# Projections pa and pb of a hybrid trunk: from plain block products to seven products per column pair, in sequence with the gates

## The reference

```python
hn = rms_norm(h, norm_g[l])
z = jnp.einsum("btd,dn->btn", hn, w_in[l])
xa, sa, vb, gb, sb, ma, mb = jnp.split(z, SPLIT_IDX, axis=-1)
ya = rg_lru(causal_depthwise_conv(xa, ...), ...) * jax.nn.silu(sa)
pa = jnp.einsum("btc,cd->btd", ya, w_proj_a[l])
yb = causal_depthwise_conv(vb * jax.nn.sigmoid(gb), ...)
yb = jax.nn.silu(layer_norm(yb, ...)) * jax.nn.silu(sb)
pb = jnp.einsum("btc,cd->btd", yb, w_proj_b[l])
merged = jax.nn.sigmoid(ma) * pa + jax.nn.sigmoid(mb) * pb
h = h + jnp.einsum("btd,de->bte", merged, w_out[l])
out = rms_norm(h, final_g)
```

## Time and profile before

| | |
|---|---|
| median of 3 runs | 1823.39 us |
| profiled execution | 1824.23 us |
| its span, first to last instruction | 1822.7 us |
| TensorE busy with matmuls | 1791.8 us (98%) |
| weight loads | 1646.7 us (90%) |
| VectorE | 1279.1 us (70%) |
| ScalarE | 666.3 us (37%) |
| DMA, mean over the span | 127 GB/s |

### The profile page before, as it was taken

The page is one execution under the profiler, slowest core; times in us unless marked ns, Lnnn a source line. Parts: engine busy times, 40 slices in busy tenths (PEclk is TensorE's granted clock), DMA queues, the critical chain, the costliest instruction groups (busy, mean ns, idle before and its releaser), DMA issues.

```text
span 1822.7 us, 28896 instructions
## 1 busy us (share of the span) xinstructions
PE 1791.8 (98%) x11732; PEld 1646.7 (90%) x11732; DVE 1279.1 (70%) x1610; ACT 666.3 (37%) x838; POOL 120.8 (7%) x134
## 2 busy tenths in 40 slices
PE   7999999999999999999999989999999999999998
PEld 7899999999999999988999989999888888888886
DVE  7969797979798888888888767888633333333431
ACT  5542424242424242423444444545422222222322
POOL 5400000000000000000000000000000000000000
PEclk9999999999999999999999999999999999999999
DMA  5233333333323233244444424444644433336422
GB/s 186 74 110 94 110 95 107 104 98 104 109 92 109 93 107 101 89 145 162 153 161 150 149 96 152 155 156 144 208 168 153 136 116 116 124 108 219 144 88 93
DMA packets 177888, 231.31 MB, mean 127 GB/s; under 512 B 6416, under 2 KB 154000, under 8 KB 177168
## 3 DMA queue, kind: packets, MB, share of 16 engines
q1 hardware_dynamic: 164800, 180.87, 30.6%
q0 software_dynamic: 13008, 49.29, 8.0%
HBM read 204.97 MB, written 25.17 MB: 126 GB/s over the span
## 4 chain that ended last, share of the span: by engine, by line
PE 87%; issue 7%; DVE 4%; ACT 1%; DMA 1%; POOL 0%; SPq 0%; POOLq 0%; ACTq 0%; DVEq 0%
PE psum L532 60%; PE psum L566 15%; PE psum L719 7%; PE psum L733 2%; PE psum L623 1%; DVE x_lo L1197 1%; DVE w_lo L1090 1%; DVE region L1516 1%; DMA aux<-conv_b_spill 0%; DMA region<-in_x_channels 0%; DVE region L1166 0%; ACT w_hi L748 0%; DVE w_lo L1324 0%; POOL aux L440 0%; POOL conv_b_spill L436 0%
## 5 line engine op out<-in xcount | busy, mean ns | idle before, releaser
L532 PE MATMUL psum<-x_hi,w_hi 128*128 128x264 f32 (+1 forms) x2144 | 553.0, 316 | 8.5 <-ACT w_hi L748 3.8
L532 PE MATMUL psum<-x_lo,w_hi 128*128 128x264 f32 (+1 forms) x2144 | 552.0, 316 | 0.0
L532 PEld LDWEIGHTS psum<-x_hi,w_hi 128*128 128x128 f32 x2144 | 353.7, 189 | 36.1 <-issue 7.3
L532 PEld LDWEIGHTS psum<-x_lo,w_hi 128*128 128x128 f32 x2144 | 353.5, 188 | 25.9 <-issue 0.2
L532 PE MATMUL psum<-x_hi,w_lo 128*128 128x264 f32 (+1 forms) x2144 | 354.8, 315 | 2.0 <-DVE w_lo L1090 2.0
L532 PEld LDWEIGHTS psum<-x_hi,w_lo 128*128 128x128 f32 x2144 | 308.3, 188 | 28.3 <-DVE w_lo L1090 2.4
L1112 DVE SCALAR_TENSOR_TENSOR region<-region,conv_cols 128x512 f32<-128x512 f32 x480 | 326.7, 747 | 0.0
L748 ACT ACTIVATE w_hi<-raw 128x1024 fp32r<-128x1024 f32 x128 | 135.7, 1060 | 435.7 <-PE psum L532 399.4
L1315 DVE TENSOR_TENSOR w_lo<-raw,w_hi 128x1024 fp32r<-128x1024 f32 x76 | 93.1, 1224 | 211.4 <-ACT w_hi L893 211.4
L1090 DVE TENSOR_TENSOR w_lo<-raw,w_hi 128x1024 fp32r<-128x1024 f32 x128 | 161.1, 1259 | 58.8 <-ACT w_hi L748 58.6
L893 ACT ACTIVATE w_hi<-raw 128x1024 fp32r<-128x1024 f32 x76 | 80.6, 1061 | 301.3 <-PE psum L532 273.2
(11 more groups left out here) (209 smaller groups left out, 2779.0 us busy)
## 6 DMA issues: line engine op xcount, KB each, us to landing
raw<-in_w_in SPq DMA_DIRECT2D x140, 512.0 KB, 3.5
region<-in_w_in SPq DMA_DIRECT2D x42, 1024.0 KB, 5.1
raw<-in_w_proj_a SPq DMA_DIRECT2D x32, 512.0 KB, 3.3
raw<-in_w_proj_b SPq DMA_DIRECT2D x32, 512.0 KB, 3.3
raw<-in_w_out SPq DMA_DIRECT2D x32, 512.0 KB, 3.8
aux<-conv_b_spill POOLq DMA_DIRECT2D x24, 512.0 KB, 4.5
region<-in_x_channels SPq DMA_DIRECT2D x8, 512.0 KB, 7.8
gated_a_spill<-wide POOLq DMA_DIRECT2D x8, 512.0 KB, 3.2
```

Source lines behind the costliest of these rows:

```text
L532: last = pe.matmul(psum[:, bank, 0:width], weights[:, s, k, m * P:(m + 1) * P], operand[part][:, place(4 * group + k), t0:t0 + width], sta ...
```

## The change

- pa and pb become units too: `NV = 5 * PAIRS - 3` = 37. Stage 4 is gone. `w_source` gives the weights; the channels of y are paired so that one of a pair of tiles is the first half of the inner dimension and the other the second.
- The tokens of pa and pb are needed as three blocks of y and four token sums. In the bodies VectorE forms the sums of ya (`ya_t_sums`, four operations of 128x256) at position 0 and `t_sums` moves to position 6; `TAPS` puts one more tap at position 0. GpSimd's queue spills seven blocks (`operand_spill`) with four DMAs for each body in place of one. For yb the sums are formed in the units of sb (`yb_t_sums`, four operations of 128x256).
- At the two places where the tokens change (`SWITCH`: v = 21, the first unit of pa, and v = 29, the first of pb) each of the seven token operands is loaded (1 MB, SyncE's queue) once the same product of the unit before is done; it lands in the `lo` tile, ScalarE cuts `hi` (`operand_hi_of`, 128x2048) and VectorE `lo` (`operand_lo_of`, 128x2048).
- The products of a unit run in another order: S1, S2, A12, S3, then A11 of the *next* unit, then A22, S4. ScalarE writes minus the first product into bank b (`seed`), and products S2, S3 and A22 accumulate onto it; `u2` and `u3` are now plain reads by ScalarE, which also reads C21. VectorE keeps C22 and C12.
- The inverse deviation of the layer norm is spread over units 10 to 12; before, it stood in unit 9. The centred tiles are spilled, so that `centre` runs once for each pair of tiles.
- The gated pa goes to HBM; the gated pb is added to it there by an accumulating DMA (`spill_o`, last branch); `load_merged` fetches the sum and the cut is made in place.
- In front of unit 0, A11 is cut before the last gate of stage 2.

```diff
-        STD, NV = 3, 3 * PAIRS - 3
+        STD, NV = 3, 5 * PAIRS - 3
-        A0 = W0 + 7 * NV
-        B0 = A0 + 4 * PAIRS
-        O0 = B0 + 4 * PAIRS
+        O0 = W0 + 7 * NV
+        UNIT = (S1, S2, A12, S3, A11, A22, S4)
...
+        SWITCH = {PA * PAIRS - STD: 0, PB * PAIRS - STD: 1}
...
+            def load_operand(v, q):
+                n = SWITCH[v]
...
+                sp.wait_ge(multiplied, chunk(v - 1, q) + 1)
+                sp.dma_start(token_operand(q)[1].bitcast(F32), operand_spill[n][spilled_block(q)])\
+                    .then_inc(operand_loaded[q], 16)
...
+            for v in range(1, NV):
+                switch = v - 1 in SWITCH
+                if switch:
+                    load_operand(v - 1, A11)
+                load_blocks(v, 0)
+                if switch:
+                    for q in (S1, S2, A12):
+                        load_operand(v - 1, q)
+                load_blocks(v, 1)
+                if switch:
+                    for q in (S3, A22, S4):
+                        load_operand(v - 1, q)
...
+                    pool.dma_start(pair_rows(m_spill, i), o, accum_op=ALU.add).then_inc(done, 16)
...
+                product(v, S1, bank_of(v, 2), False)
...
+                pe.wait_ge(seeded, v + 1)
+                product(v, S2, bank_of(v, 1), True)
+                product(v, A12, bank_of(v, 0), True)
+                pe.wait_ge(u2_ready, v + 1)
+                product(v, S3, bank_of(v, 1), True)
+                if v + 1 < NV:
+                    first_product(v + 1)
                 pe.wait_ge(u3_ready, v + 1)
+                product(v, A22, bank_of(v, 1), True)
                 pe.wait_ge(c22_ready, v + 1)
+                product(v, S4, bank_of(v, 2), True)
...
+            def seed(v):
+                act.wait_ge(multiplied, chunk(v, A11) + 1)
...
+                act.activation(bank(v, 1), bank(v, 0), ACT.Copy, scale=-1.0).then_inc(seeded, 1)
+
+            def read_u2(v):
+                act.wait_ge(multiplied, chunk(v, S2) + 1)
+                wait(act, c12_ready, v)
+                act.activation(u2, bank(v, 1), ACT.Copy, scale=-1.0).then_inc(u2_ready, 1)
...
+            def operand_lo_of(v, q):
+                dve.wait_ge(operand_hi, 7 * SWITCH[v] + SWITCH_ORDER.index(q) + 1)
+                hi, lo = token_operand(q)
+                dve.tensor_tensor(lo, lo.bitcast(F32), hi.bitcast(F32), ALU.subtract).then_inc(operand_lo, 1)
...
-            TAPS = [0, 3, 3, 3, 3, 1, 1, 3, 2, 3, 2, 3, 3, 1, 0, 0]
+            TAPS = [1, 3, 3, 3, 3, 1, 1, 3, 2, 3, 2, 3, 2, 1, 0, 0]
```

More of the change, by code:

```diff
@@ new lines, in chunk, with w_source @@
+        def chunk(v, q):
+            if q == A11:
+                return W0 + 7 * v - 2 if v else W0
+            return W0 + 7 * v + 1 + (UNIT.index(q) - (v == NV - 1 and q in (A22, S4)))
+        def w_source(w):
+            kind, i = divmod(w, PAIRS)
+            if kind in (PA, PB):
+                view = (w_pa_v if kind == PA else w_pb_v).rearrange("p (k h) n -> p h k n", h=2)
+                return [view[:, h, :, 256 * i:256 * i + 256] for h in range(2)]
+            column = (COL_MA, COL_MB, COL_SB)[kind] + 256 * i
+            return [w_in_v[:, KH * h:KH * (h + 1), ds(column, 256)] for h in range(2)]
@@ new lines, in spilled_block, with spills, y_place @@
+        def spilled_block(q):
+            return {A11: B11, A12: B21, S4: B22, S1: T_BLOCKS + T_N1, S2: T_BLOCKS + T_T2, S3: T_BLOCKS + T_T3,
+                    A22: T_BLOCKS + T_T4}[q]
+        SWITCH = {PA * PAIRS - STD: 0, PB * PAIRS - STD: 1}
+        SWITCH_ORDER = (A11, S1, S2, A12, S3, A22, S4)
+        def spills(w):
+            return sum(32 if n // PAIRS == SB else 16 for n in range(w % 2, w, 2))
+        def y_place(j):
+            return 4 * (T_N1, T_T2, T_T3, T_T4)[j // 4] + j % 4
@@ L505, in _ @@
+            load_merged(PAIRS - 1)
+            pool.wait_ge(lo_ready, O0)
             for t in range(TT):
@@ L508, in _ @@
                 pool.dma_start(tokens[:, t, :], x_v[t]).then_inc(x_reloaded[t], 16)
+            for n in range(2):
+                pool.wait_ge(o_spilled[n], spills(5 * PAIRS + n))
             pool.wait_ge(multiplied, O0 + 2 * TT + 1)
@@ L591, in unit @@
                     pe.wait_ge(c11_ready, v - 1)
-                product(v, A11, a, x_block(0, 0), False)
-                wait(pe, c21_ready, v - 1)
+                product(v, A11, bank_of(v, 0), False)
+            def unit(v):
+                wait(pe, c12_ready, v - 1)
+                wait(pe, c22_ready, v - 1)
                 if v == 0:
@@ L936, in gate_rest, with gate_c21 @@
+            def gate_c21(v):
+                w = STD + v
+                act.wait_ge(multiplied, chunk(v, A22) + 1)
+                wait(act, o_spilled[w % 2], spills(w))
+                act.activation(o_slots[:, w % 2, 1, 0:HS], bank(v, 1), gate_of(v)).then_inc(c21_ready, 1)
             def gate_rest(v):
                 w = STD + v
-                act.wait_ge(c22_ready, v + 1)
-                act.wait_ge(c21_ready, v + 1)
-                act.wait_ge(c12_ready, v + 1)
-                rest = o_flat(w)[:, HS:]
```

724 lines of the change are left out of this document (352 added, 372 removed).

## The result

The changed kernel takes **1834.22 us**, median of 4 runs (1832.09 to 1836.11), against 1823.34 (1823.23 to 1824.08) for the kernel before on the same chip: ratio **1.0058**, 95% interval 1.0044 to 1.0073. It is 0.6% slower, and the whole interval lies above 1; 1806 was forecast, and the range ended at 1822.

What follows compares the result with a forecast made beforehand. TensorE, at work in 98% of the span, was taken to bound the kernel. 1824.23 - 32.3 - 12.9 + 2.8 + 1.0 + 20.4 + 2 + 2 = 1807.2 for the profiled execution, 1806 as median; range 1791 to 1822.

Steps and rivals of the forecast that it cites:

- Part 1: pa and pb: 16 plain pairs become 16 units of 19.92 us, in full on TensorE's path, -32.3 us.
- Part 2: Stage 3: TensorE's stalls at its head and around the variance's root and reciprocal go, -12.9 us.
- rival (d): Units 10 to 12: root and reciprocal still hold TensorE, +9.6 us, 1816; chance 0.07.
- Part 4: Stage 2: the added sums make the cut of the third chunk late, +1.0 us.
- Part 7: Margins: table loads around ScalarE's root and handoffs between engines over 37 units, +2 us.
- rival (b): All 37 units: each loses 0.5 us in handoffs between engines, 1823, no change; chance 0.12.
- Part 3: Bodies: added VectorE work makes the first gate operand 0.4 us late in seven bodies, +2.8 us.
- Part 5: The two switches: VectorE's extra operand cuts make it late, 13.6 us at the first and 6.8 at the second.
- gaps at the switches that end with loads: Sign named beforehand: the forecast would be wrong if TensorE's gaps at the switches ended with loads.
- rival (c): Switches: transfers hold them up, 52.8 us in place of 20.4, 1839, slower than before; chance 0.07.
- Part 6: Clock: TensorE resumes at 1.2 GHz after long stalls, +2 us for all.
- The output projection, forecast as nothing: Start of the output projection: the last merged pair is needed 38 us after the first, so no cost.

Runs made afterwards that it cites:

- run 8: Changed kernel with the bodies' token sums later (VectorE's `t_sums` at position 9 instead of 6, ScalarE's `t_hi_of` at 11 instead of 8): 1831.2 us.
- run 1: Changed kernel with only the first 128 KB of each 1 MB token-operand load fetched, all cuts whole: 1819.3 us.
- run 2: Changed kernel with loads whole, but ScalarE and VectorE cutting only an eighth of each token operand: 1813.1 us.
- run 3: Changed kernel with both token-operand loads and their cuts shortened to an eighth: 1796.6 us.
- run 5: Changed kernel with SyncE's order at a switch altered: S1 and S2 operands before the next unit's first weight half, S3 and A22 before the second: 1824.4 us.
- run 7: Changed kernel with GpSimd's first two reloads of x issued before the last spill of pb: 1829.6 us.
- The fastest kernel: Changed kernel plus SyncE's new load order, weights cut before operands, earlier x reloads, later token sums, and C22 read earlier beside switches: 1806.9 us.
- run 12: The fastest kernel with only the first eighth of each token operand loaded: 1797.8 us.

## Why the prediction was wrong

**Right.** Part 1: 1536 matmuls last 182.24 us, and 16 pairs became 16 units of 19.92; the row's pitch held, and that of the Trainium skill ("TensorE: Matmul & The Clock Gate", Part 1) would have promised 6 us more. Part 2: the units follow stage 2 without a gap, and the chain has no stall around the reciprocal; rival (d) fell. Part 4: +0.9 for 1.0 (765.04 to 861.65, where 760.14 to 855.81 stood before). Part 7: no unit outside the switches lost anything worth a line (1.3 us in all); rival (b) fell.

**Part 3, mis-sized: 4.6 for 2.8.** The wait in front of the first gate round was 0.43 us in the chain for 0.4, and the six matmuls of the round took 0.97 us there instead of 0.74: 0.66 in each of seven bodies (0.2 us more lie ahead of them), and with run 8 the period is back. The step left out the overlap that a gap takes away. It counted from 453.45, where the chain of before has the round; the timeline has its first matmul at 453.28, ahead of the modelled end of the matmul in front.

**Part 5, the failing step.** It priced the switches at VectorE's backlog alone, 20.4 us, and put the transfers at nothing beside it. They cost at least 14.9 us. The prediction had named the sign: gaps at the switches that end with loads. Two sentences of rival (c) carried that step. The first was "7.5 late, which is within what VectorE costs anyway". It took the later of two delays. But an operand's load, ScalarE's cut and VectorE's cut are one chain on one pair of buffers, and the load starts only when the last product has read them (`wait_ge(multiplied, ...)` in `load_operand`). In the first switch VectorE stands idle for 10.23 us while it waits and does its extra work afterwards. The two add: runs 1, 2 and 3 have 14.9 + 21.1 against 37.6. The second was "3.3 us for 1 MB when loads overlap". That is what the engines of the DMA move in a time; what a chain waits for is the time from issue to landing, and that was 10.6 and 12.0 us. Loads of operands and weights and the spills of yb were in flight together (389 and 408 GB/s at a share of 1.0 in the windows above), and three loads were issued behind weights that waited for VectorE; mending that order alone gave 9.8 us (run 5).

Part 5's count of VectorE came near: with the transfers short, TensorE waits 14.3 us at the first switch for 13.6 forecast and 5.8 at the second for 6.8. Some of that is luck. The waits behind late short loads are in it, 3.8 us stay with short cuts too (run 3), and the step's own terms for the first switch (9 x 1.13 + 2 x 2.2 + 4 x 0.415 + 3.5) make 19.7 and not 20.5.

Rival (c) had a mechanism that acts, and 0.07 was too small a chance for it. That its 1839 is nearer to the result than the forecast is mostly luck. It had nine loads run one at a time and VectorE's backlog hidden behind them; in the run the loads overlapped and the two added. Its 6.8 us for one load is a time from load to load and not one from issue to landing, so the 10.6 and 12.0 us are no test of it (and by its own sum the kernel is as slow as before from 6.4 us).

**Part 6, mis-sized: 12.9 for 2.** As a term of the sum this is the largest miss: 10.9 us, where the waits missed by 8.1 (28.5 for 20.4). Part 6 counted four stalls and took 2 us for all of them, where the earlier trace rows had 1.7 for one. There were eleven waits of up to 5.5 us in the window, and five stretches at 0.50 of the clock. Even the 7 us for four such stalls was low. The clock's part goes with the waits: of the lost time it is 26 to 39% in every row of the table. With short loads it is still 7.7 us, which together with the output projection and the bodies is why run 1 stays 13 us above the forecast. The rule of the Trainium skill ("TensorE: Matmul & The Clock Gate", Part 1), that a longer idle gap brings the low clock back, agrees with these windows. In the first switch they have 0.56, 0.55 and 0.51 around the end of the waits of 4.7, 3.6 and 5.5 us and behind it, and 1.00 behind those of 0.3 to 2.6 us.

**The output projection, forecast as nothing, cost 4.5.** "The last merged pair is needed 38 us after the first" was about the pair, and it was on time. What was not looked at was who else loads there: `w_out` took 5.9, 9.6 and 6.6 us in the chain, beside reloads of the merged tiles, of x and the last spill. With two reloads of x moved, run 7 wins 2.7 us of it back in its trace (177.0 us for 179.7, and 175.1 before). What the other 1.9 are is not shown, but for 0.8 us in which TensorE waits in front of its first matmul.

**What stays open.** The fastest kernel still loses 25.6 us around the switches: 10.8 go with the transfers (25.6 - 14.8), and by run 3 most of the rest with the operands' cuts, which were not tried with short cuts in the new order. Whether another DMA queue for the operands would help was not tried either.

## What to carry to other kernels

Before two delays at one place are compared and the larger taken, ask whether they lie on one chain: here load, cut and product of one buffer added up, and an engine that stood for a load did its backlog afterwards. Price a load that something waits for from issue to landing with all the traffic of that moment beside it, not by the bandwidth, and look at what is queued behind the waiting instruction on each engine: here moving loads, cuts, sums and one read past a wait took 27 us of 1834 without leaving any work out. And where TensorE will wait several times in a row, add for the clock: here 0.4 to 0.6 of the waits again.

## What was not expected of the hardware

- Short transfers beside long ones are not short in proportion: in run 1 the four `t_lo` loads of 128 KB still took a median of 8.0 us from issue to landing, those of `x_lo` 2.6. In the order of run 12 `t_lo` took 2.5 and `x_lo` 4.0 (DMA views of 1250 to 1335, run 1 first):

```profile
t_lo<-ya_operand SPq DMA_DIRECT2D x4, 128.0 KB, 8.0
...
x_lo<-ya_operand SPq DMA_DIRECT2D x3, 128.0 KB, 2.6
```

```profile
t_lo<-ya_operand SPq DMA_DIRECT2D x4, 128.0 KB, 2.5
```

- A gap costs more than the chain shows as its wait: 0.43 us in front of six matmuls lengthened the body by 0.66. From start to start the six took 0.81 us for 0.74; the rest is the overlap of 0.17 us of a matmul with the modelled end of the one in front, which the gap takes away.
- The low clock added nearly half of the waits again: 12.9 us beside 28.5 us.
